# The last channel chunk of the sample's depthwise convolution computed on POOL as products and sums during attention, in a one-layer encoder kernel

## What is computed

```python
def encoder_layer(x, ...):
    h = rms_norm(x, attn_norm_g)
    proj = h @ w_in
    q, k, v, cv, cg = jnp.split(proj, ...)            # cv, cg: 512 channels each
    q = apply_rope(rms_norm(q, q_norm_g), cos, sin)
    k = apply_rope(rms_norm(k, k_norm_g), cos, sin)
    attn = blocked_attention(q, k, v)                 # 8 heads, blocks of 128 queries
    conv = conformer_conv(cv, cg, conv_dw_w, conv_dw_b, conv_ln_g, conv_ln_b)
    mixed = jnp.concatenate([rms_norm(attn, attn_out_g), rms_norm(conv, conv_out_g)], axis=-1)
    x = x + mixed @ w_out
    return x + expert_choice_ffn(rms_norm(x, ffn_norm_g), w_router, w_gate, w_up, w_down)

def conformer_conv(cv, cg, dw_w, dw_b, ln_g, ln_b):
    u = cv * jax.nn.sigmoid(cg)
    u = depthwise_conv(u, dw_w, width=31, centred) + dw_b   # out[t] = b + sum_k w[k] * u[t + k - 15]
    return jax.nn.silu(layer_norm(u, ln_g, ln_b))
```

## Time and profile before

| | |
|---|---|
| median of 3 runs | 2606.68 us (2606.09 to 2607.51) |
| the profiled execution's own time | 2606.63 us |
| its span, first to last instruction | 2604.8 us |
| PE busy | 2547.3 us (98%) |
| DVE busy | 1822.1 us (70%) |
| ACT busy | 1396.3 us (54%) |
| POOL busy | 274.6 us (11%) |
| granted TensorE clock, mean | 0.995 |

### The profile page before, as it was taken

One profiled execution on the slowest core, in us unless ns is written; L12 is line 12 of the kernel. 1 busy time (PEld: TensorE's weight loads), 2 busy tenths in 40 slices (PEclk: granted clock), 3 DMA queues, 4 the chain that ended last, 5 costly groups with the idle time before them and its releaser, 6 DMA issues.

```text
span 2604.8 us, 40071 instructions
## 1 busy us (share of the span) xinstructions
PE 2547.3 (98%) x16030; PEld 2351.1 (90%) x16030; DVE 1822.1 (70%) x2088; ACT 1396.3 (54%) x1762; POOL 274.6 (11%) x269
## 2 busy tenths in 40 slices
PE   8999999998998999999999999999999999999998
PEld 8889899977887999989999898998989999899997
DVE  7878899975466766767666676666767667676664
ACT  4232666677223555656555565554655556555563
POOL 3735100000000000101001010110101101010010
PEclk9999999999998999999999999999999999999999
DMA  7344000012226677867778787787868768787774
GB/s 248 103 173 162 9 1 1 1 57 91 105 106 204 232 237 236 255 228 254 227 255 252 226 255 227 246 248 240 254 223 257 239 234 257 228 257 225 247 240 125
DMA packets 339357, 499.40 MB, mean 192 GB/s; under 512 B 10224, under 2 KB 287088, under 8 KB 337264
## 3 DMA queue, kind: packets, MB, share of 16 engines
q1 hardware_dynamic: 332144, 471.76, 54.9%
q0 software_dynamic: 7040, 25.17, 3.9%
HBM read 457.05 MB, written 39.85 MB: 191 GB/s over the span
## 4 chain that ended last, share of the span: by engine, by line
PE 89%; DVE 6%; ACT 2%; POOL 1%; DMA 1%; issue 1%; SPq 0%; POOLq 0%; ACTq 0%; DVEq 0%
PE psum L1744 31%; PE psum L1746 14%; PE psum L1436 8%; PE psum L1438 8%; PE psum L1437 8%; PE psum L1767 4%; PE psum L1766 4%; PE psum L1597 4%; PE psum L1573 2%; PE psum L1584 2%; DVE conv L989 2%; PE psum L1671 1%; DVE smx L1094 1%; DVE q_st L1084 1%; ACT probs L750 1%
## 5 line engine op out<-in xcount | busy, mean ns | idle before, releaser
L1335 DVE TENSOR_TENSOR w_lo<-raw,w_hi 128x2048 fp32r<-128x2048 f32 x384 | 880.1, 2292 | 482.4 <-ACT w_hi L875 479.8
L1744 PE MATMUL psum<-xgT,w_hi 128*128 128x384 f32 x4096 | 1168.8, 360 | 2.4 <-issue 2.4
L1746 PE MATMUL psum<-xgT,w_lo 128*128 128x192 f32 x4096 | 1026.6, 251 | 0.0
L875 ACT CAST w_hi<-raw 128x2048 fp32r<-128x2048 f32 x384 | 733.5, 1910 | 322.5 <-PE psum L1767 319.6
L1746 PEld LDWEIGHTS psum<-xgT,w_lo 128*128 128x128 f32 x4096 | 783.9, 191 | 0.6
L1744 PEld LDWEIGHTS psum<-xgT,w_hi 128*128 128x128 f32 x4096 | 770.5, 188 | 3.2 <-issue 2.6
L989 DVE SCALAR_TENSOR_TENSOR conv<-conv,colp 128x1024 f32<-128x1024 f32 (+1 forms) x240 | 252.7, 1053 | 4.8
L1436 PE MATMUL psum<-w_hi,hid_st 128*128 128x512 f32 x512 | 210.2, 411 | 0.0
L1438 PE MATMUL psum<-w_hi,hid_st 128*128 128x512 f32 x512 | 200.0, 391 | 0.0
L1437 PE MATMUL psum<-w_lo,hid_st 128*128 128x512 f32 x512 | 199.9, 390 | 0.0
L1767 PE MATMUL psum<-w_lo,hid_st 128*128 128x512 f32 x508 | 198.2, 390 | 0.0
(11 more groups left out here) (217 smaller groups left out, 3370.5 us busy)
## 6 DMA issues: line engine op xcount, KB each, us to landing
raw<-in_w_gate_dram SPq DMA_DIRECT2D x128, 1024.0 KB, 5.3
raw<-in_w_up_dram SPq DMA_DIRECT2D x128, 1024.0 KB, 5.3
raw<-in_w_down_dram SPq DMA_DIRECT2D x128, 1024.0 KB, 4.9
wi_raw<-in_w_in_dram SPq DMA_DIRECT2D x28, 256.0 KB, 5.2
wi_kept<-wi_hi SPq DMA_DIRECT2D x14, 512.0 KB, 6.1
wi_kept<-wi_lo SPq DMA_DIRECT2D x14, 512.0 KB, 6.5
wi_hi<-wi_kept SPq DMA_DIRECT2D x7, 1024.0 KB, 4.7
wi_lo<-wi_kept SPq DMA_DIRECT2D x7, 1024.0 KB, 7.3
```

Source lines behind the costliest of these rows:

```text
L875: act.copy(w_hi[:, j % SPLIT_SLOTS, :], raw[:, j % RAW_SLOTS, :]).then_inc(e_hi, 1)
L1335: dve.tensor_tensor(w_lo[:, j % SPLIT_SLOTS, :], raw[:, j % RAW_SLOTS, :], w_hi[:, j % SPLIT_SLOTS, :].bitcast(F32), ALU.subtract).then_in ...
L1744: pe.matmul(bank[:, 0:2 * CAP], w_hi[:, slot, w0:w0 + P], xgT[:, half, k, :], start=(k == 0), stop=False, skip_group_check=True)
L1746: last = pe.matmul(bank[:, 0:CAP], w_lo[:, slot, w0:w0 + P], xgT[:, half, k, 0:CAP], start=False, stop=(k == KD - 1), skip_group_check=True)
```

## The change

POOL gets a list of 61 instructions behind its last rotary step: the 31 taps of chunk 3 of the sample. The first is `tensor_scalar` with product and bias in one; each of the other 30 is a product (`tensor_scalar`, one tensor input) into a scratch tile `pool_product` and a sum (`tensor_tensor`, two SBUF inputs) into the result. Each waits for the one before it (`pool_tap`). Result and scratch are tiles 11 and 10 of `conv_tok`, which are free until `conv_rows` writes them. DVE's list of taps loses these 31: it keeps 124 prompt and 93 sample taps. The rule for the prompt units becomes two instead of three sample taps where u is a multiple of 3, so that the 93 stand in units 26 to 61 and none is left for the sample units. PE's sample transposes wait for `pool_tap` and take chunk 3 from POOL's result. The semaphore `c_var` is folded into `c_bn`.

```diff
-        TAPS = [(0, c, k) for c in range(NC_CONV) for k in range(CONV_K)] + [(1, c, k) for c in range(NC_CONV) for k in range(CONV_K)]
+        POOL_CHUNKS = (3,)
+        POOL_STEPS = 2 * CONV_K - 1
+        TAPS = [(g, c, k) for g in range(2) for c in range(NC_CONV) if g == 0 or c not in POOL_CHUNKS for k in range(CONV_K)]
+        pool_rows = {3: conv_tok[:, TILES - 1, :], 2: junk[:, :]}
+        pool_product = conv_tok[:, TILES - 2, :]
...
+            pool.wait_ge(consts_in, 32)
+            pool.wait_ge(glu_u, len(GLU_BLOCKS))
+            for n, c in enumerate(POOL_CHUNKS):
+                out = pool_rows[c]
+                for k in range(CONV_K):
+                    _, u, tap = conv_operands(1, c, k)
+                    done = POOL_STEPS * n + 2 * k - 1
+                    if done > 0:
+                        pool.wait_ge(pool_tap, done)
+                    if k == 0:
+                        pool.tensor_scalar(out, u, tap, colp[:, COL_BIAS + c:COL_BIAS + c + 1], ALU.mult, ALU.add
+                                           ).then_inc(pool_tap, 1)
+                    else:
+                        pool.tensor_scalar(pool_product, u, tap, None, ALU.mult).then_inc(pool_tap, 1)
+                        pool.wait_ge(pool_tap, done + 1)
+                        pool.tensor_tensor(out, out, pool_product, ALU.add).then_inc(pool_tap, 1)
...
-                dve.wait_ge(c_bn, 2 * t + 1)
+                dve.wait_ge(c_bn, 3 * t + 1)
...
                 if u < PROMPT_UNITS:
-                    conv_run(3 - turns if sample_next else 2 - (turns or u % 4 == 0))
+                    conv_run(3 - (turns or u % 3 == 0) if sample_next else 2 - (turns or u % 4 == 0))
                 elif u < PROMPT_UNITS + 2 * ROT_TILES - 2:
                     conv_run(1)
...
+                if g == 1:
+                    pe.wait_ge(pool_tap, POOL_STEPS * len(POOL_CHUNKS))
                 for c in range(NC_CONV):
-                    last = pe.transpose(psum[:, 1 + 2 * (t % 2), c * P:(c + 1) * P], conv[:, c, col:col + P], ident[:, :])
+                    i = (t - GROUPS[g][0]) * P
+                    rows = pool_rows[c][:, i:i + P] if g == 1 and c in POOL_CHUNKS else conv[:, c, col:col + P]
+                    last = pe.transpose(psum[:, 1 + 2 * (t % 2), c * P:(c + 1) * P], rows, ident[:, :])
```

More of the change, by code:

```diff
@@ L239, in encoder_layer_kernel @@
         t_rstd = sem("t_rstd"); t_norm = sem("t_norm"); rope_a = sem("rope_a"); rope_b = sem("rope_b"); rope_c = sem("rope_c")
-        v_ok = sem("v_ok"); conv_tap = sem("conv_tap");
+        v_ok = sem("v_ok"); conv_tap = sem("conv_tap"); pool_tap = sem("pool_tap")
         q_T = sem("q_T"); k_T = sem("k_T"); q_hi = sem("q_hi"); k_hi = sem("k_hi"); q_lo = sem("q_lo"); k_lo = sem("k_lo")
@@ L245, in encoder_layer_kernel @@
         wo_h = sem("wo_h"); wo_l = sem("wo_l"); rows_in = sem("rows_in")
-        lngb_in = sem("lngb_in"); cT = sem("cT"); c_bn = sem("c_bn"); c_var = sem("c_var"); c_cen = sem("c_cen"); a_sq = sem("a_sq")
+        lngb_in = sem("lngb_in"); cT = sem("cT"); c_bn = sem("c_bn"); c_cen = sem("c_cen"); a_sq = sem("a_sq")
         c_std = sem("c_std"); c_rstd = sem("c_rstd"); c_ln = sem("c_ln"); c_act = sem("c_act"); c_sq = sem("c_sq")
@@ L787, in _ @@
                 if u == NORM_UNIT:
-                    act.wait_ge(c_var, TILES)
+                    act.wait_ge(c_bn, 3 * TILES)
                     act.activation(cst[:, C_STD, :], cst[:, CV, :], ACT.Sqrt).then_inc(c_std, 1)
@@ L1107, in conv_rows @@
                 dve.bn_stats(bst[:, t, 0:6], rows_ps).then_inc(c_bn, 1)
-                dve.wait_ge(c_bn, 2 * t + 1)
+                dve.wait_ge(c_bn, 3 * t + 1)
                 dve.bn_aggr(bst[:, t, 6:8], bst[:, t, 0:6]).then_inc(c_bn, 1)
-                dve.wait_ge(c_bn, 2 * t + 2)
-                dve.tensor_scalar(cst[:, CV, t:t + 1], bst[:, t, 7:8], EPS, None, ALU.add).then_inc(c_var, 1)
+                dve.wait_ge(c_bn, 3 * t + 2)
+                dve.tensor_scalar(cst[:, CV, t:t + 1], bst[:, t, 7:8], EPS, None, ALU.add).then_inc(c_bn, 1)
                 dve.scalar_tensor_tensor(out=conv_tok[:, t, :], in0=rows_ps, scalar=bst[:, t, 6:7], in1=lngb[:, 0, :],
```

## The result

| | before | after |
|---|---|---|
| median | 2606.68 us | 2611.9 us |
| runs | 13: twelve of 2604.07 to 2609.09, one of 3051.92 | 13, 2608.23 to 2620.52 |
| the profiled execution's own time | 2606.63 us | 2609.98 us |
| its span | 2604.8 us | 2608.2 us |
| DVE busy | 1822.1 us | 1809.6 us |

The ratio of the times, after to before, is 1.0024 with a 95% interval of 1.0016 to 1.0032: the change makes the kernel slower by 4 to 8 us.

The account below looks back on a forecast made before the run. PE, busy in 98% of the span, was taken to bound the kernel. A 4.6 us gain in sample units and a 7.0 us loss from POOL beside DVE gave +2.4 us, 2609.0 us, in a range of 2602.5 to 2624.

Parts of the forecast that it names:

- The prompt's 18 taps: Prompt units: removing 18 sample taps of 0.77 us from DVE is worth nothing, since PE fills those units.
- PE's wait: At unit 80, near 558.85 us, PE's new wait for POOL's chain is hidden by about 150 us.
- The gain: Sample units: seven pairs without taps last 4.56 us each, 31.92 instead of 36.51 us, saving 4.6 us.
- The loss: Attention units 5 to 25: POOL's products and sums hold up DVE's taps, costing 7 us.
- second cycle: Two-tap units: the sum waits behind the first tap and delays the second, costing 0.95 us a unit.
- rival (b): A POOL product excludes DVE's taps for its whole length, like a sum: +15, 2622 us; chance 0.30.
- Half and half: The 16 two-tap units split evenly between both POOL patterns: 8 x 0.2 + 8 x 0.95 = 9.2 us lost.
- the regained 2 us: Some 2 us of POOL's cost to DVE is regained where DVE now waits for PE.
- first cycle: Two-tap units: the sum runs beside the maximum and ends too late for the next tap, costing 0.2 us a unit.
- likely part: The likely part of the main forecast's own time range: 2603 to 2614 us.
- Rival (a): In attention, POOL costs DVE next to nothing, 0 to 1 us: 2602 to 2603 us; chance 0.15.
- Rival (c): The 4.6 us don't come: another wait, say `conv_rows`, keeps sample pairs at 5.2 us; 2611 us, chance 0.05.

Follow-up runs that it names:

- e7: Against the changed kernel, ACT's eight squares of the prompt's attention rows moved from units 68 to 75 to units 88 to 95; 2612.49 us, one run.
- e6: Against the changed kernel, each POOL sum replaced by a second product of the same shape, so chunk 3 is wrong; 2609.07 us.
- e5: Against the changed kernel, each POOL product released behind a unit's taps, each sum with the next unit's first tap; 2622.85 us.
- e3: Against the changed kernel, POOL paced to one instruction a unit, each waiting for that unit's taps, work complete; 2603.59 us.
- a0: The changed kernel run again without edits, beside the kernel before; 2611.09 us, ratio 1.0024 to before.
- e1: Against the changed kernel, POOL's 30 products and sums left out, only its first tap done; 2602.39 us.
- e8: Against the changed kernel, POOL's whole chain held back until the last prompt tap is done, at unit 26; 2608.26 us.
- e11: Against the changed kernel, the first of POOL's thirty product-sum pairs held until the taps of unit 5 are done, then free; 2615.49 us.

## Why the prediction came out as it did

- **The place of gain and loss: right.** Most of the loss lies in units 5 to 27 in two cycles, the gain in the sample units. The prompt's 18 taps and the merged semaphore brought nothing. PE's wait was hidden by 178 us (I had said 150), and POOL's chain was over at 384.6 (385 to 400).
- **The gain: the term was too large by 1.0 us**, 3.6 instead of 4.6 for the seven pairs. The step that failed is the choice of the pair at 554 us as the price for all seven. It has no squares on ACT: the taps had hidden a second delay, which became the next one in four of the seven pairs and took 0.7 us, as e7 shows. And it has no prompt unit on PE, as the first pair has, which took 0.36; that is read from PE's rows and not tested. The 0.3 us at unit 64, which I had put at 0.1 or 0.2 and not counted, made the gain 3.9 after all.
- **The loss: 7.9 us instead of 7.** The second cycle's price was right (0.91 for 0.95). The first one's, 0.31 for 0.2, was nearly right in size but had the wrong cause: I put it down to a sum that ends late; e6 shows the product's hold. In the earlier trace rows I had the bound for it, "at most 0.6 us", and used it only against rival (b), not as a price in the cycle where a product starts as the first tap ends.
- **"Half and half", 9.2 us, was too dear, and the regained 2 us were too hopeful.** Ten two-tap units ran in the first cycle, three in the second and two between them, not eight and eight, and of the five one-tap units the two with turns, 16 and 20, moved POOL from cycle to cycle. The early turn units cost 0.3 us up to unit 6. By the shift 3.3 us were lost up to unit 18, in the first cycle, 4.3 from 18 to 26, mostly in the second, and 0.3 after; nothing was given back before unit 64. The two errors nearly cancelled, so that the 7.9 lies near the forecast's 7 is in part luck. The range was also wide, 21.5 us, and the measured median stands exactly on the limit, 2611.9, that the forecast had drawn between no difference and slower. Its "likely part", 2603 to 2614, reaches below its own lower end of 2605: the ends leave out the regained 2 us, the likely part doesn't.
- **Rival (b) refuted** by e6. The page "SBUF — State Buffer" of the Trainium skill, section "Who interferes with whom", says that whoever issues first keeps the other out for the whole instruction. The runs agree for the sum (taps of 2.2 us in e5) and for the product that waits behind a tap (2.57 us); they disagree for the product in front, 0.3 us on the next tap, and there the measurement decides.
- **Rival (a)**, POOL at next to no cost, is what pacing makes (e3), not what the change did. **Rival (c)** was true for 1.0 of its 4.6 us, through ACT and PE and not through `conv_rows` alone.
- **What remains.** The sum was made for the profiled execution and said +2.4; by the shifts attention became 4.1 us longer (4.2 in a0), and the profiled execution's time rose by 3.4. The medians rose by 5.2 and, in the second series, 5.8. The intervals of the ratios are 4.2 to 8.3 and 3.6 to 8.9 us, so 4.1 stands at their lower end, and the few runs near 2619 raise the upper. e1's median, 2.9 us under before's, has an interval of 0.5 to 5.5 us, with its profile's 3.8 inside. Whether a microsecond is lost outside attention these measurements can't tell.

## What to carry to other kernels

Work moved to an idle engine that shares a memory with the busy one is priced by its meetings, not by its duration: the same 61 instructions cost 19, 8 or 0.5 us, according to which of DVE's instructions they meet. Semaphores are not the only place where engines meet: no semaphore joins POOL's chain to the taps in the changed kernel. Tie each instruction to a point of the busy engine's list behind which comes something it does not disturb (here a maximum from PSUM), and don't let a chain run free: here it stayed in one phase for ten units and more. And when a delay of several tenths is removed from a stage, look on every other engine of the same units, not in a neighbouring stretch, for what is late next.

## What the runs showed of the hardware that I had not expected

- A POOL product (`tensor_scalar`, one SBUF input, factor from a column, 512 columns, 1.56 us alone) shuts a two-input DVE instruction out for about its first 0.6 us only, an estimate: the tap behind it takes 1.6 us instead of 1.28 (e6: 21 times, never more). Products that had not waited bear it out in the changed kernel: a tap that started 0.36 us into one (277.67 and 277.31 us) took 1.40, one that started 0.49 us into one (349.40 and 348.91) took 1.28, so that the hold is over by some 0.7 us. Behind such a DVE instruction it waits in full (2.57 us).
- The first one, with product and bias both from columns, took 0.76 us, half of a product:

```profile
270.42 0.76 POOL L598 TENSOR_SCALAR conv_tok<-conv,colp 128x512 f32<-128x512 f32 x1
271.27 1.56 POOL L601 TENSOR_SCALAR conv_tok<-conv,colp 128x512 f32<-128x512 f32 x1
```

  In e8 the same instruction, at unit 26, took 0.77, so its place in time is not the cause. Whether the second operand makes it faster, or the place of tap 0 in the row, was not tried.
- A DVE tap with one tensor input (line 1018 of e3) took 1.17 us beside a product where it takes 0.81 in before; the maximum from PSUM kept its 1.20 to 1.23 us beside products and sums.
- Two engines that merely wait for each other's instructions settled into a repeating pattern that outlived its cause: one wait at unit 5 (e11) set the price of the next ten units, up to the turn at unit 16.
